# Who subtracts the weight slabs of two attention layers: GpSimd (before), VectorE (after)

## What is computed

```python
for l in range(2):
    h  = ffn_half(h, ml, 0, ...);  hc = ffn_half(hc, mc, 0, ...)
    hn = modulate(rmsnorm_2(h, norm_g[l, 1]), ml[3], ml[4])      # hcn likewise from hc
    qa, ka, va, qb, kb, vb, uc, gl = project_tokens(hn, w_in[l], qk_g[l], cos, sin)
    ya = softmax attention of 8 heads;  yb = difference of two softmaxes, 4 heads;  yc = fourier_mix(uc)
    h  = h + ml[5] * merge_branches(ya, yb, yc, gl, w_branch[l], w_out[l])
    h  = ffn_half(h, ml, 2, ...)                                 # hc only in layer 0
```

## Time and profile before

| | |
|---|---|
| median of 3 runs | 3220.3 us (3219.12 to 3221.1) |
| the profiled execution | 3223.55 us, its span 3221.7 us |
| PE busy | 92% of the span |
| DVE busy | 49%, 2154 instructions |
| ACT busy | 32% |
| POOL busy | 14%, 241 instructions |
| mean granted TensorE clock | 0.957 of full speed |

### The profile page before, as it was taken

How to read it: one execution, slowest core, us unless ns; L and a number is a source line. 1 busy time by engine, 2 the same in 40 slices (tenths; PEclk the granted TensorE clock), 3 DMA queues, 4 the chain that set the end, 5 groups by cost and what they waited for, 6 DMA issues and landing times.

```text
span 3221.7 us, 54730 instructions
## 1 busy us (share of the span) xinstructions
PE 2949.1 (92%) x23653; PEld 2385.3 (74%) x23653; DVE 1573.8 (49%) x2154; ACT 1031.2 (32%) x1502; POOL 459.0 (14%) x241
## 2 busy tenths in 40 slices
PE   6998877999999889899899989999899998988899
PEld 6776564677667689776578768888688877678899
DVE  6534243233232366672755444445544457476466
ACT  3221213222222254432642332222422224353443
POOL 5123000000000000131134400000000012246200
PEclk9998888999999989899999999999999998999899
DMA  6346858998889845311012222222222222113452
GB/s 241 131 176 245 332 230 332 414 377 354 363 348 372 369 146 190 121 66 40 1 53 105 92 106 103 91 92 99 71 92 101 95 79 79 40 53 145 182 186 89
DMA packets 77066, 547.78 MB, mean 170 GB/s; under 512 B 8384, under 2 KB 10432, under 8 KB 11056
## 3 DMA queue, kind: packets, MB, share of 16 engines
q1 hardware_dynamic: 76000, 540.05, 43.4%
q0 software_dynamic: 848, 4.52, 0.4%
HBM read 637.86 MB, written 1.05 MB: 198 GB/s over the span
## 4 chain that ended last, share of the span: by engine, by line
PE 79%; DVE 11%; ACT 4%; DMA 4%; issue 2%; POOL 1%; SPq 0%; DVEq 0%; POOLq 0%; ACTq 0%
PE bank L743 56%; PE bank L1087 9%; DMA ring<-slabs 3%; PE bank L1409 2%; DVE clow L2471 1%; PE bank L792 1%; ACT whi L1853 1%; ACT ht L1657 1%; DVE tiny L2624 1%; PE bank L922 1%; PE bank L1497 1%; PE bank L909 1%; PE bank L759 1%; DVE wk L2601 1%; PE bank L1478 1%
## 5 line engine op out<-in xcount | busy, mean ns | idle before, releaser
L743 PE MATMUL bank<-hhi,whi 128*128 128x256 f32 (+1 forms) x1408 | 481.9, 342 | 30.7 <-DVE hlo L2105 30.7
L743 PE MATMUL bank<-hlo,whi 128*128 128x256 f32 (+1 forms) x1408 | 476.6, 338 | 0.0
L743 PE MATMUL bank<-hhi,wlo 128*128 128x256 f32 (+1 forms) x1408 | 472.9, 336 | 0.0
L2085 DVE TENSOR_TENSOR wlo<-ring,whi 128x2048 fp32r<-128x2048 f32 x132 | 298.7, 2288 | 223.9 <-ACT whi L1612 197.0
L743 PE MATMUL bank<-fhl,whi 128*128 128x256 f32 (+1 forms) x1408 | 351.6, 341 | 0.0
L1612 ACT ACTIVATE whi<-ring 128x2048 fp32r<-128x2048 f32 x132 | 251.3, 1908 | 212.0 <-PE bank L743 211.3
L743 PEld LDWEIGHTS bank<-hhi,whi 128*128 128x128 f32 x1408 | 266.8, 189 | 70.6 <-issue 29.6
L743 PEld LDWEIGHTS bank<-hhi,wlo 128*128 128x128 f32 x1408 | 268.0, 190 | 30.3
L743 PEld LDWEIGHTS bank<-hlo,whi 128*128 128x128 f32 x1408 | 268.2, 191 | 26.3
L1087 PE MATMUL bank<-ring,wk 128*32 128x256 f32 x4064 | 256.2, 396 | 21.6 <-DMA ring<-slabs 12.9
L723 POOL TENSOR_TENSOR wlo<-ring,pw 128x2048 fp32r<-128x2048 f32 x22 | 101.4, 4609 | 1192.5 <-ACT pw L1618 1192.5
(11 more groups left out here) (477 smaller groups left out, 5535.7 us busy)
## 6 DMA issues: line engine op xcount, KB each, us to landing
ring<-slabs SPq DMA_DIRECT2D x542, 1024.0 KB
wk<-slabs SPq DMA_DIRECT2D x45, 1024.0 KB, 11.6
ac<-slabs SPq DMA_DIRECT2D x16, 1024.0 KB, 11.1
wk<-mixp POOLq DMA_DIRECT2D x1, 1040.0 KB, 12.4
xt<-xT SPq DMA_DIRECT2D x1, 1024.0 KB, 6.3
xt<-ctxT POOLq DMA_DIRECT2D x1, 1024.0 KB, 6.0
out<-xt SPq DMA_DIRECT2D x4, 256.0 KB, 2.4
cst<-maskc POOLq DMA_DIRECT2D x1, 960.0 KB, 14.4
```

The lines of the kernel that those rows point to most:

```text
L743: last = pe.matmul(o, a, b, start=k == 0, stop=k == len(pairs) - 1)
L2085: tt_(wlo_of(n), slab(n), whi_of(rel).bitcast(F32), ALU.subtract).then_inc(sem("wlo"), 1)
```

## The change

POOL's loop goes. DVE gets `att_low(l, i)`, with the same two waits, the same operands and the same semaphore, at places written out by hand: two in the norm ahead of the wait for `sd`; slabs 2 to 7 ahead of the scaling of tiles 2, 4, 5, 7, 9 and 11; slabs 8 to 10 behind the rotation of the last tile; 11 and 12 in attention jobs 6 and 8; 13 behind the last job; the rest behind the products of the merge; the last three behind the merge. Nothing changes on PE, ACT and SP.

```diff
--- before.py
+++ after.py
@@ -715,13 +715,6 @@
             pool.wait_ge(sem("mo"), 1)
             pool.dma_start(cst[:, 0:NCA], attc).then_inc(sem("attin"), 16)
 
-            for l in range(2):
-                for i in range(N_ATT):
-                    n = att_slab(l, i)
-                    slab_wait(pool, n)
-                    pool.wait_ge(sem("aw"), count("aw", N_ATT * l + i + 1))
-                    pool.tensor_tensor(wlo_of(n), slab(n), att_whi(l, i).bitcast(F32), ALU.subtract
-                                       ).then_inc(sem("al"), 1)
 
 
         @block.tensor
@@ -2084,6 +2077,13 @@
                 slab_wait(dve, n, i, 3 * un // NSLOT)
                 tt_(wlo_of(n), slab(n), whi_of(rel).bitcast(F32), ALU.subtract).then_inc(sem("wlo"), 1)
 
+            def att_low(l, i):
+
+                n = att_slab(l, i)
+                slab_wait(dve, n)
+                dve.wait_ge(sem("aw"), count("aw", N_ATT * l + i + 1))
+                tt_(wlo_of(n), slab(n), att_whi(l, i).bitcast(F32), ALU.subtract).then_inc(sem("al"), 1)
+
             def norm(n, T, ph=None, h0=None, high=None):
 
                 if n >= 3:
@@ -2094,6 +2094,9 @@
                     then(tt_(AMOD, AMOD, w.to_broadcast([P, 8, 2]), ALU.mult))
                 if ph is not None:
                     split_slab(ph, 0)
+                elif n >= 4:
+                    for i in range(2):
+                        att_low(l, i)
                 dve.wait_ge(sem("sd"), n + 1)
                 then(dve.reciprocal(rs[:, 0:T], rs[:, 0:T]))
                 if n >= 3:
@@ -2593,7 +2596,10 @@
                 tiles = qk_tiles(l)
                 q0 = 13 * l
                 dve.wait_ge(sem("attin"), 16)
+                due = {2: 2, 4: 3, 5: 4, 7: 5, 9: 6, 11: 7}
                 for i in range(14):
+                    if i in due:
+                        att_low(l, due[i])
                     if i < 13:
                         t, _, _, T, row = tiles[i]
                         r = RQ[i % 2][:, 0:T]
@@ -2608,6 +2614,8 @@
                         tt_(RTMP[i % 2], bank[4 + (i - 1) % 2][:, 0:TX], ca["sin"], ALU.mult)
                         then(tt_(x, x, ca["cos"], ALU.mult))
                         tt_(x, x, RTMP[i % 2], ALU.add).then_inc(sem("qd"), 1)
+                for i in range(8, 11):
+                    att_low(l, i)
                 f0 = 8 * l
                 for n in range(4 * (tq // TX)):
                     dve.wait_ge(sem("f2"), f0 + n + 1)
@@ -2664,11 +2672,17 @@
                     if n + 1 < len(js):
                         maxima(n + 1)
                     scale(n)
+                    if n == 6:
+                        att_low(l, att_gate(0))
+                    if n == 8:
+                        att_low(l, att_branch(0))
                     if n:
                         result(n - 1)
                     if na + 1 < n <= na + 5:
                         branch_low(0, n - na - 2)
                 result(len(js) - 1)
+                att_low(l, att_gate(1))
+
                 def sub_norm(h):
                     dve.wait_ge(sem("ysd"), 4 * l + h + 1)
                     r, x = YS[h][:, 0:tq], QK[:, 5 + h, 0:tq]
@@ -2692,9 +2706,17 @@
                         branch_low(1, n - 4)
                     if 10 <= n < 14:
                         branch_low(2, n - 10)
+                    if n % 2 and n < 21:
+                        att_low(l, att_gate(2 + n // 2))
+                    if n % 4 == 2 and n < 20:
+                        att_low(l, att_branch(n // 4 + 1))
                     if n >= 17:
                         merged_low(n - 17)
+                    if n == 21:
+                        att_low(l, att_wout(0))
                 merged_low(7)
+                for m in range(1, 4):
+                    att_low(l, att_wout(m))
                 for j in range(8):
                     dve.wait_ge(sem("wo2"), 8 * l + j + 1)
                     for half in range(tq // TX):
```

## The result

The changed kernel takes 3233.8 us, the median of 16 runs (3227.9 to 3240.1), beside 3220.5 for the kernel before (16 runs, 3215.9 to 3230.9). The ratio is 1.0036, 95% interval 1.0028 to 1.0044: slower by about 12 us (the medians differ by 13.3). The forecast was 3232.3 with a range of 3221 to 3241, slower.

What follows compares the result with a forecast made beforehand. PE, busy 92%, was taken as the bound, with DVE at 49%. Terms 15.9 + 11.9 - 4.0 - 10.9 + 1.0 gave +13.9, less 2 made +12: median 3220.3 to 3232.3 us, range 3221 to 3241.

Steps and rivals of the forecast that it cites:

- Slab by slab, layer 0: Projections of layer 0: new PE waits of 1.0 (slab 2), 7.8 (3), 3.6 (4 to 7), 3.5 (8); +15.9 us.
- Layer 1: Norm and projections of layer 1: +2.0 us in the norm, +5.7 at slab 3, +3.5 at slab 8; sum +11.9.
- Merge of layer 1: Merge of layer 1: DVE's work fits, and PE's waits of 7.0 and 3.9 us go; -10.9 us.
- Jobs: Attention jobs: subtractions cost about 1.3 us each, old waits of 3.7 and 5.5 go; -1.1 and -2.9, sum -4.0 us.
- Clock: Half clock behind PE's stalls: some 12 us go with old waits, 13 come with new ones; net +1.0 us.
- six at 2.2: Clock loss of new waits over 2 us: six stalls at 2.2 us each, 13 us in all.
- The 2 us taken off for small terms: Taken off +13.9, giving +12, since a delayed PE gives DVE back some slack at the next tile.
- DVE at 51 to 52%: Whole kernel, a sign of being right: DVE busy near 49 + 4.6 - 2 = 51 to 52%.
- Rival A: Slab 3 is released before tile 5, so no big wait; -4.6 us, or 3211 with small waits hidden; chance 8%.
- Rival B: New stalls cost no half clock and the old 12 us come back: +1, 3221 us, no change; chance 12%.
- rival C: DVE bounds more places: job subtractions count in full, clock stays down for two stretches; +26, 3246 us; chance 12%.
- the signs named: Waits at tile 5 and slab 8, later norm reciprocal, short DVE operations, full layer 1 merge, feed-forward unchanged.

Runs made afterwards that it cites:

- e1: The change with slab 3 alone moved on DVE ahead of tile 3's scaling instead of tile 4's, both layers; 3221.5 us, 0.9994 of the kernel before.
- e2: The change with DVE's projection subtractions one tile earlier and one of the norm's two behind the norm, both layers; 3199.3 us, 0.9934 of the kernel before.
- e6: The kernel of e2 with slab 3 alone back ahead of tile 4's scaling, both layers; 3212.4 us, 0.9970 of the kernel before.
- e3: The change with POOL keeping the 11 norm and projection slabs of each layer; 3196.7 us, 0.9931 of the kernel before; 3201.6 on the repeat.
- e7: The change with 16 unused POOL subtractions (two SBUF operands) added in the merge of layer 1; 3268.8 us, 1.0157 of the kernel before.
- e8: The change with 16 unused POOL additions of a constant (one SBUF operand) added in layer 1's merge; 3255.1 us, 1.0102 of the kernel before.
- e5: The kernel of e2 with POOL keeping layer 0's 11 norm and projection slabs; 3201.5 us, 0.9936 of the kernel before; 3200.1 on the repeat.

## Why the prediction was right, and where not

- **Slab by slab, layer 0: right.** The waits are 0.98 (slab 2), 7.85 (slab 3), 0.54, 0.98, 0.98, 0.98 (slabs 4 to 7) and 3.51 us (slab 8): 15.8 for the 15.9 of the sum. e1 showed for slab 3 that the place was the cause, e2 for all.
- **Layer 1: right in kind, 1 to 2 us low.** The two subtractions of the norm stand ahead of the reciprocal, 4.4 us; PE's wait for the first product is 9.99 us, 2.2 more than the 7.78 before (2.0 in the sum):

```profile
2661.45 4.49 DVE L2085 TENSOR_TENSOR wlo<-ring,pw 128x2048 fp32r<-128x2048 f32 x2 [0.29 <-DVE tiny L2094]
2665.86 3.34 DVE L2101 RECIPROCAL rs<-rs 128x512 f32<-128x512 f32 x1
```

Slabs 2, 3, 7 and 8 cost 1.28, 5.82, 0.98 and 3.51 (1.2, 5.7, 1.1, 3.5 in the sum). The step that failed is "slabs 5 and 6 about 0, since DVE catches up": slab 5 had a wait of 2.07. Slab 4 was put at 0 too; its wait is 2.62 where one of 3.78 went, so it came out 1.2 too high. PE's idle time rose by 10.9, where the terms behind the norm make 9.9.
- **Merge of layer 1: the idle time of 10.9 us went, to the tenth.** The clock gave 7.2 us more in this stage, which the sum has in its clock term.
- **Jobs: right sign, too small.** -4.0 was the term; PE's idle time fell by 2.1 and 4.2, so 6.3. Against the 3.7 and 5.5 that went, the new subtractions cost about 1.6 and 1.3 where the sum had 2.6 in each layer. The reading that DVE has "about 0.9 us per job free" compares one stretched instruction with one wait and is not a measured idle time.
- **Clock: +1.0 in the sum; PE's busy time fell by 0.8 over the five stretches** (+4.2, -3.1, +4.0, +1.3, -7.2). Near, but with both parts too large: 13 in and 12 out in the sum, 9.5 in and 10.3 out by stage. And a fixed price per stall ("six at 2.2") is refuted. Behind the wait of 7.85 us stand 5.8 us at half clock, a loss of 2.8:

```profile
1399.20:1405.00 5.80, 5.78 (x14) 4.53 (x15) 0.00 (x0) 1.91 (x1) 0.00 (x0) 0.51 0.47 181
```

The same wait lost 1.4 in e6 (its projections of layer 0 took 9.2 us more for 7.8 of wait), and that of 3.51 us lost nothing in the change and, with 5.4 busy microseconds at 0.50, 2.7 in e1. And the jobs of layer 0 have 0.99 in the change and 0.95 before (3.1 us of busy time). One stall of 3.7 us went there, but e3, where PE is idle for 19.2 us in this stage beside 19.7 in the change, has 0.96.
- **The 2 us taken off for small terms** were meant for slack that DVE gets back. They came out for other reasons, so that the total meets 12.0 so closely is luck: jobs -2.3, clock -1.8, projections of layer 1 +1.0, the stretch with the norm +0.8, the rest +0.5, layer 0's projections -0.1. That makes the 12.0 from 13.9.
- **DVE at 51 to 52%: wrong**, it stayed at 49%. I had counted 49 + 4.6 - 2. The 2% of stretching was too low: DVE's unchanged total shows that it was as much as the work added, 151 us.
- **Rival A** (the big wait does not come) was e1 on the chip. By its terms the sum falls by 18.5, of which 5 are clock; it fell by 12.3, and the time is that of the kernel before, since the half clock moved to another stall. With the smaller waits gone too I had priced it at 3211; e2 is at 3199, 12 lower. That price left the two waits of 3.5 us at slab 8, the 2.0 of the norm and 2.3 for slabs 2 and 7 of layer 1 in place, 11.3 us, and e2 took these away as well.
- **Rival B** is excluded by the interval, **rival C** by the jobs: no wait of PE for DVE there is over 1.9 us, and the half clock behind the longest stall lasts 5.8 us, not twice 5.4.
- **Of the signs named**, the waits, the norm's reciprocal, the full merge and the short operations came (L2615, L2704 and L2661 stay under 0.7 us). The stretches with the feed-forward stages grew by 0.6 us beyond the norm's 2.2, and by 0.5.

## What to carry to other kernels

Moving work to an engine that is twice as fast and half idle cost 12 us here, because each piece was put behind an instruction that waits; the same work at places one tile earlier (and one of the norm's two behind the norm) left the kernel 21 us faster than before. Before an instruction is put into an in-order queue, look for the longest idle stretch ahead of it and ask whether its own operands were there when that began. And POOL's cost is not what PE waits for it, but what it stretches on DVE: give POOL its share in the stages in which PE is full anyway, and take it away where DVE's small operations feed PE.

## What the runs showed of the hardware

- 16 POOL operations of 3.6 to 7.5 us each whose results nobody uses cost 35 and 25 us in the merge of layer 1 (e7 and e8). Plus a constant (one SBUF operand) took POOL 6.18 us in the mean for 128x2048, against 4.12 for the subtraction in e7 (4.61 in the kernel before).
- In the two kernels profiled twice (e3 and e5), the execution repeats to 0.1 us in 1850 from the first projection on; their 5.3 and 5.2 us of scatter lie ahead of it.
- One stage with the same source for all engines took 129.0 or 137.0 us in two kernels, each number reproducible, with a granted clock of 0.96 and 0.89. So a gain of under 8 us in this kernel can't be put down to an edit by the total alone.
